# One more place for expert weights, a norm by token tile, and a scale vector loaded as rows, in a two-layer hybrid trunk

## The reference

```python
def rms_norm(x, g):
    y = x * lax.rsqrt(jnp.mean(x * x, axis=-1, keepdims=True) + EPS)
    return y * g

for i in range(2):
    h = rms_norm(x, norm_mix_g[i])
    mix = s5_mixer(h, ...) if i == 0 else diff_attention(h, w_qkv, ...)   # q, k, v = split(h @ w_qkv, 3)
    x = x + mix
    h = rms_norm(x, norm_ffn_g[i])
    x = x + hier_moe(h, ...)
return rms_norm(x, final_norm_g)
```

## Time and profile before

| | us |
|---|---|
| median of 3 runs | 857.2 (854.8 to 857.51) |
| the profiled execution | 857.5 |
| its span, first to last instruction | 855.0 |
| TensorE busy | 726.0 |
| VectorE busy | 262.4 |
| ScalarE busy | 194.3 |
| mean granted TensorE clock | 0.932 |
| transfers | 236.32 MB, mean 276 GB/s |

### The profile page before, as it was taken

The page is one execution under the profiler, slowest core; times in us unless marked ns, Lnnn a source line. Parts: engine busy times, 40 slices in busy tenths (PEclk is TensorE's granted clock), DMA queues, the critical chain, the costliest instruction groups (busy, mean ns, idle before and its releaser), DMA issues.

```text
span 855.0 us, 15847 instructions
## 1 busy us (share of the span) xinstructions
PE 726.0 (85%) x6433; PEld 434.5 (51%) x6435; DVE 262.4 (31%) x765; ACT 194.3 (23%) x451; POOL 48.8 (6%) x48
## 2 busy tenths in 40 slices
PE   4997799989977667657999988888989999987896
PEld 4987554565543333423544544475545555544453
DVE  6868971143111011002223354425101111111112
ACT  5674603241111010002102232324101111111012
POOL 3693000000000000000000000000000000000000
PEclk9998799979999798888999998989999999999898
DMA  9632209685999999999931670061999920999991
GB/s 240 186 109 96 104 7 387 230 357 236 424 424 424 422 424 424 424 425 395 397 144 66 230 292 3 0 245 57 412 424 420 423 87 0 401 423 425 422 394 51
DMA packets 59949, 236.32 MB, mean 276 GB/s; under 512 B 20008, under 2 KB 20208, under 8 KB 35312
## 3 DMA queue, kind: packets, MB, share of 16 engines
q1 hardware_dynamic: 57968, 235.23, 69.0%
q10 hardware_dynamic: 1920, 0.24, 0.2%
HBM read 234.41 MB, written 1.05 MB: 275 GB/s over the span
## 4 chain that ended last, share of the span: by engine, by line
PE 58%; SPq 17%; DMA 12%; DVE 5%; ACT 5%; issue 2%; ACTq 0%; DVEq 0%
SPq L402 15%; PE ps L1713 10%; PE ps L1778 10%; DMA ring<-in_moe_w_down 8%; PE ps L1631 6%; PE ps L1748 6%; PE ps L1755 5%; PE ps L1695 4%; DMA work<-in_moe_w_down 3%; PE ps L1502 2%; PE ps L1841 2%; PE ps L1472 2%; PE ps L1851 2%; PE ps L1662 1%; DMA work<-in_norm_mix_g 1%
## 5 line engine op out<-in xcount | busy, mean ns | idle before, releaser
L1713 PE MATMUL ps<-ring,work 128*32 128x256 f32 x1600 | 113.6, 416 | 34.9 <-DMA ring<-in_moe_w_up 22.8
L1713 PEld LDWEIGHTS ps<-ring,work 128*32 128x32 f32 x1600 | 63.2, 120 | 78.1 <-issue 55.4
L1292 DVE TENSOR_TENSOR work<-ps,work 128x256 f32<-128x256 f32 x21 | 12.9, 615 | 292.6 <-PE ps L1713 292.6
L1713 PE MATMUL ps<-work 128*32 128x256 f32 x992 | 81.9, 413 | 22.6 <-DMA work<-in_moe_w_up 11.5
L1755 PE MATMUL ps<-work 128*128 128x512 f32 x168 | 77.7, 605 | 0.0
L1748 PE MATMUL ps<-ring,work 128*32 128x512 f32 x512 | 69.1, 595 | 8.7 <-DMA ring<-in_moe_w_down 5.9
L1713 PEld LDWEIGHTS ps<-work 128*32 128x32 f32 x992 | 43.5, 119 | 59.0 <-issue 37.2
L1695 PE MATMUL ps<-work,xr 128*128 128x128 bf16 x736 | 66.6, 219 | 2.2 <-DVE work L1242 2.2
L1695 PE MATMUL ps<-work 128*128 128x128 bf16 x368 | 63.9, 219 | 0.0
L1695 PEld LDWEIGHTS ps<-work,xr 128*128 128x128 bf16 x736 | 56.5, 98 | 12.8 <-issue 8.6
L1778 PE MATMUL ps<-ring,hT 128*128 128x512 f32 x128 | 56.4, 595 | 1.7 <-ACT hT L555 1.7
(11 more groups left out here) (311 smaller groups left out, 967.6 us busy)
## 6 DMA issues: line engine op xcount, KB each, us to landing
ring<-in_moe_w_gate SPq DMA_DIRECT2D x24, 2048.0 KB, 25.0
ring<-in_moe_w_down SPq DMA_DIRECT2D x23, 2048.0 KB, 21.0
work<-in_moe_w_up SPq DMA_DIRECT2D x15, 2048.0 KB, 22.7
ring<-in_moe_w_up SPq DMA_DIRECT2D x15, 2048.0 KB, 22.8
work<-in_moe_w_down SPq DMA_DIRECT2D x8, 2048.0 KB, 27.3
work<-in_moe_w_gate SPq DMA_DIRECT2D x7, 2048.0 KB, 19.7
ring<-in_ssm_w_glu SPq DMA_DIRECT2D x4, 2048.0 KB, 8.9
ring<-in_attn_w_qkv SPq DMA_DIRECT2D x4, 2048.0 KB, 26.3
```

The source lines that it names most:

```text
L1713: ins = mm(ps[s, 6 + j // 2, 0:256], xg[:, k, s], pairs[slots[e // 2]][e % 2][:, k, :], start=(k == 0), stop=(k == KD - 1))
```

## The change

Four edits, which touch different stages:

- The scale vector of norm 0 is loaded as 8 rows of 128 into `grow`; TensorE turns it into bank 7 (one transpose ahead of `turn()`, behind a wait for the load), and ScalarE copies 8 columns to `gq[:, 0, :]`. VectorE and ScalarE wait for that copy instead of the load.
- Norm 2 goes by token tile, as norms 1 and 3 do, into banks 6, 7 (tile 0) and 4, 5 (tile 1). TensorE turns tile 0, runs `project(0, 0)`, turns tile 1, and goes on with `project(0, 1)`. `project(0, 4)` waits for hT of both tiles.
- An eleventh place, slot 10 (`SPLIT1`), is put together from x and hT. It is used in layer 1, from unit 65 on; its first use waits for `x_free`, which `residual(l, 1, 1)` raises in each layer. A unit of layer 1 from 65 on lies where the unit ten before it lay.
- `turn` and `norm` lose what was there for norm 2; the last norm is as before.

```diff
-SLOTN = 10
+SLOTN = 11
+SPLIT1 = 10
@@ slot_plan
-    order, used, plan = [(s, None) for s in TURNS] + [(LATE, None), (SPLIT, None)], list(DENSE), []
+    order, used, plan = [(s, None) for s in TURNS] + [(LATE, None), (SPLIT, None), (SPLIT1, None)], list(DENSE), []
     for i in range(2 * 6 * NQ + 8):
-        at = next(n for n, (s, _) in enumerate(order) if not (s == LATE and i in dense) and not (s == SPLIT and i >= 6 * NQ))
+        at = next(n for n, (s, _) in enumerate(order) if not (s == LATE and i in dense) and not (s == SPLIT and i >= 6 * NQ) and not (s == SPLIT1 and i <= 6 * NQ + 16))
         if i == 6 * NQ + 16:
             at = next(n for n, (s, _) in enumerate(order) if s == LATE)
+        if i == 6 * NQ + 17:
+            at = next(n for n, (s, _) in enumerate(order) if s == SPLIT1)
...
-        TURN_AT = {1: (4, 6), 3: (0, 6)}
+        TURN_AT = {1: (4, 6), 2: (6, 4), 3: (0, 6)}
...
+        halves.append((x[:].rearrange("p a n -> p (a n)"), hT[:].rearrange("p k t -> p (k t)")))
@@ SyncE, freed(i)
                     if slot == SPLIT:
                         sp.wait_ge(h_back, 4)
+                    if slot == SPLIT1:
+                        sp.wait_ge(x_free, 2)
@@ ScalarE
-            dma(gq[:, 0, :], a["norm_mix_g"][0].rearrange("(k q) -> q k", k=KD), s_gain0)
+            dma(grow[0:8, :], a["norm_mix_g"][0].rearrange("(k q) -> k q", k=KD), s_gain0)
...
             def norm(i, first):
 
                 act.activation(small[:, 40:41], con[:, C_TURN:C_TURN + 1], ACT.Sqrt)
+                act.wait_ge(scat1, first)
                 for tt in range(TT):
-                    if tt == 0:
-                        act.wait_ge(scat1, first)
-                    elif i == 2:
+                    if i == 2 and tt == 1:
                         act.wait_ge(x_new, 1)
                     square(tt, total_S[tt])
-                act.wait_ge(var_ready, VARS[i])
-                act.activation(small[:, 12:14], small[:, 10:12], ACT.Sqrt).then_inc(root_ready, 1)
-                if i < 4:
-                    act.wait_ge(hT_psum, TURNED[i])
-                    keep_turned(i, 4)
+                    if i == 2:
+                        root_tile(2, tt)
+                if i == 2:
+                    keep_tile(2, 0)
+                    keep_tile(2, 1)
+                else:
+                    act.wait_ge(var_ready, VARS[i])
+                    act.activation(small[:, 12:14], small[:, 10:12], ACT.Sqrt).then_inc(root_ready, 1)
...
-            act.wait_ge(s_gain0, 16)
+            act.wait_ge(g_psum, 1)
+            act.copy(gq[:, 0, :], ps[:, 7, 0:KD]).then_inc(g_kept, 1)
+            act.wait_ge(g_kept, 1)
             keep_turned(0, 0)
@@ VectorE, end of moe(0)
                     dve.tensor_copy(x[:, 1, :], total_S[1]).then_inc(x_new, 1)
-                    dve.wait_ge(squares, 5)
+                    var_tile(2, 0)
                     dve.tensor_copy(x[:, 0, :], total_S[0]).then_inc(x_new, 1)
                     dve.wait_ge(x_new, 2)
+                    norm_tile(2, 0)
+                    var_tile(2, 1)
+                    norm_tile(2, 1)
+                    keep_tile(2, 0)
+                    keep_tile(2, 1)
@@ TensorE
             pe.wait_ge(s_con, 16)
-            turn(0)
+            pe.wait_ge(s_gain0, 16)
+            pe.transpose(ps[:, 7, 0:KD], grow[0:KD, :], ident[0:KD, 0:KD]).then_inc(g_psum, 1)
+            turn()
...
-                residual(l, 1, 1)
+                residual(l, 1, 1).then_inc(x_free, 1)
...
             moe(0)
-            turn(2)
...
-            pe.wait_ge(hT_ready, 6)
-            pe.wait_ge(hT_late, 6)
+            turn_tile(2, 0)
+            pe.wait_ge(hT_ready, 5)
+            pe.wait_ge(hT_late, 5)
             project(0, 0)
+            turn_tile(2, 1)
             project(0, 1)
```

More of the change, by code:

```diff
@@ L51 @@
 SPLIT = 9
-DENSE = (2, 2, 1, 1, 0, 0, 0, 0, 0, 0)
+SPLIT1 = 10
+DENSE = (2, 2, 1, 1, 0, 0, 0, 0, 0, 0, 0)
 ITEMS = 32
@@ L197, in build @@
         GLU_ORDER = (0, 2, 1, 3)
-        TURN_AT = {1: (4, 6), 3: (0, 6)}
-        VARS = (1, 2, 4, 5, 7)
-        TURNED = (4, 5, 7, 8)
+        TURN_AT = {1: (4, 6), 2: (6, 4), 3: (0, 6)}
+        VARS = (1, 2, 4, 6, 8)
+        TURNED = (4, 5, 7, 9)
         o = 0
@@ L296, in build @@
             sem(n) for n in ("down_done", "y0_ready", "y1_ready", "scat0", "scat1"))
-        back_ready, x_new = sem("back_ready"), sem("x_new")
+        back_ready, x_new, x_free = sem("back_ready"), sem("x_new"), sem("x_free")
         qkv_done, qkv_kept, v_kept, qk_turned, qkT_ready = (
@@ L397, in whole @@
                 src = w[e0:e0 + 2, :].rearrange("e (p n) -> p e n", p=P)
-                if slot_of(i) == SPLIT:
+                if slot_of(i) in (SPLIT, SPLIT1):
                     for e in range(2):
-                        sp.dma_start(halves[SPLIT][e], src[:, e, :]).then_inc(here, 16)
+                        sp.dma_start(halves[slot_of(i)][e], src[:, e, :]).then_inc(here, 16)
                 else:
@@ L904, in norm @@
                 link(dve.reciprocal(small[:, 14:16], small[:, 12:14]))
-                if i == 2:
-                    for tt in range(TT):
-                        scale_tile(tt)
-                    keep_turned(2, 4)
-                else:
-                    dve.wait_ge(s_gain, 16)
-                    for tt in range(TT):
-                        STT(xr[:, tt, :, :].rearrange("p k q -> p (k q)"), total_S[tt], small[:, 14 + tt:15 + tt],
-                            gains[:, 1, :], ALU.mult, ALU.mult).then_inc(final_ready, 1)
+                dve.wait_ge(s_gain, 16)
+                for tt in range(TT):
+                    STT(xr[:, tt, :, :].rearrange("p k q -> p (k q)"), total_S[tt], small[:, 14 + tt:15 + tt],
+                        gains[:, 1, :], ALU.mult, ALU.mult).then_inc(final_ready, 1)
             def scale_tile(tt):
@@ L1454, in by_k, with turn @@
                 return x[:, tt, :].rearrange("p (q k) -> p k q", k=KD)
-            def turn(i):
-                pe.wait_ge(normed, 2 * i + 2)
+            def turn():
+                pe.wait_ge(normed, 2)
                 for b in range(4):
@@ L1471, in turn_tile @@
                 for k in range(KD):
-                    ins = mm(ps[:, TURN_AT[i][tt] + k // 4, P * (k % 4):P * (k % 4) + P], by_k(tt)[:, k, :], scales[:, tt, :],
+                    ins = mm(ps[:, TURN_AT[i][tt] + k // 4, P * (k % 4):P * (k % 4) + P], x[:, tt, P * k:P * k + P] if i == 2 else by_k(tt)[:, k, :], scales[:, tt, :],
                              start=True, stop=True)
@@ L1654, in residual @@
                 pe.wait_ge(mixed, 4 * l + 2 + 2 * tt)
-                mm(ps[:, 2 * tt + half, :], ident, x[:, tt, 512 * half:512 * half + 512], start=True, stop=True)
+                return mm(ps[:, 2 * tt + half, :], ident, x[:, tt, 512 * half:512 * half + 512], start=True, stop=True)
             def moe(l):
@@ L1864, in _ @@
             turn_qk(0, 2)
+            pe.wait_ge(hT_ready, 6)
+            pe.wait_ge(hT_late, 6)
             project(0, 4)
```

12 lines of the change are left out of this document (6 added, 6 removed).

## The result

The kernel after takes **845.5 us** (median of 4 runs, 844.76 to 846.87), the kernel before in the same comparison 857.17; the ratio is 0.9871, with a 95% interval of 0.9846 to 0.9897. A second comparison gave 846.27 us and 0.9886 (0.9868 to 0.9904). The forecast was 846.5. The profiled execution after has a span of 843.0 us, against 855.0 before.

The account below looks back on a forecast made before the run. The bound changes by stage; layer 1's three long passes wait 26.0 us for weights while transfers stand still in a hole. Slot 9.9, first norm 0.6 and norm 2 0.2 sum to 10.7: from 857.2 to 846.5 us, range 843.3 to 850.3.

Parts of the forecast that it names:

- The slot's mechanism: Layer 1's weight queue: waiting for the unit ten back instead of nine brings transfers earlier at two places.
- Rival (c): Train after the hole held by SyncE's order or ring, so the slot wins one unit only: 851.5 us, chance 0.08.
- third effect: Release behind the hole lets go unit 84, not 83, so group 6's last unit is 14th of its train: another 4.95 us.
- The term of 9.9 us: Eleventh slot in layer 1: two whole units of 4.95 us at 424 GB/s; bounds 4.95 and 10.4.
- a wait of 1.9 stays and the gain is the whole 4.95: Group 2's long pass: last down weight lands 640.3, wanted at 638.4, so the pass gains a full unit's transfer.
- reading of the three long passes: Layer 1 passes of 24.5, 23.4 and 30.6 us, against 17.5 undisturbed: the 26.0 us in excess is waiting for weights.
- rival (d): First norm: the scale row lands late and TensorE waits, 852.1 us at most; chance 0.05.
- the 4.1 of the estimate: First norm: landing time in us of the scale row, estimated from a transfer's fixed cost of about 2.0 us.
- the third bank's 15.00: First norm: the third bank lets VectorE go at 15.00 us, so the chain goes on at 17.35, 0.6 us earlier.
- My bounds, 0 and 1.5: First norm's scale row: limits in us around its forecast gain of 0.6.
- the gain of 1.8: Norm 2 by tile: projection 1 ends 1.8 us earlier if the clock is at 2.4 GHz from projection 0's start.
- the split gives nothing: Norm 2: by the skill page's clock rule, splitting the turn gives nothing; 0.2 us was taken, bounds 1.8 and -0.8.

Follow-up runs that it names:

- slot_only: The kernel before with the eleventh slot alone, from unit 65 on; 849.15 us, ratio 0.9917.
- slot_mid: The kernel before with the eleventh slot alone, first given to local unit 27 of layer 1, on which SyncE stands at the hole; 850.89 us, ratio 0.9938.
- slot_late: slot_only with the slot first given to local unit 28 of layer 1, the first issued after the hole; 857.0 us, ratio 1.0002.
- warm_start: turns_first with 20 unread products of zeros at the start and 10 of constants ahead of the first norm's turns; 841.68 us, ratio 0.983.
- warm_norm: turns_first with 22 unread filling products on TensorE ahead of norm 2's turns; 840.98 us, ratio 0.982.
- warm_both: turns_first with the fillings of warm_norm and warm_down, the latter in both passes of group 2; 842.88 us, ratio 0.984.
- warm_down: turns_first with 13 unread products ahead of the down-weight wait in both layer-1 passes of group 2; 841.68 us, ratio 0.9823.
- gain_only: The kernel before with norm 0's scale vector loaded as rows alone; 854.63 us, ratio 0.999.
- after_again: The kernel after run once more without an edit, in more rounds; 846.27 us, ratio 0.9886.
- turns_first: The kernel after with both of norm 2's tile turns ahead of projection 0; 841.81 us, ratio 0.9827.
- norm_only: The kernel before with norm 2 by token tile alone; 855.68 us, ratio 0.9993.
- warm_all: turns_first with warm_start's and warm_norm's fillings, and 13 products in group 2's first layer-1 pass only; 841.03 us, ratio 0.9827.

## Why the prediction was right, and where its terms were off

**The slot's mechanism was right.** Unit 65 left at 583.66, ahead of the release; group 2's last weight, the release behind the hole and group 6's last weight all came earlier, and what was late last stayed late last. Rival (c), one unit only, is out: slot_only and slot_mid show both units. My reading of the third effect, that the unit let go behind the hole is 84 instead of 83 because 83 has gone out before, is what slot_mid isolates; slot_late shows how little it takes to lose it.

**The term of 9.9 us was mis-sized: it brought 7.5 to 7.7.** The first unit brought 2.9 to 3.1 and not 4.95. Group 2's last weight did land nearly as much earlier as forecast, counted from the stage's release: 43.4 us after it in the kernel after against 48.2 before (636.05 - 592.62 and 645.2 - 596.99). Most of what is missing, 1.7 us, is the granted clock: six traces have the early slot and nothing filled in at group 2, and TensorE's down products there took 5.34 us in four of them and 3.64 in two. The step that failed is "a wait of 1.9 stays and the gain is the whole 4.95": I counted the wait's length and not what the clock does behind it. In the kernel before the wait right ahead of these products is 1.33 us long, and they keep 2.4 GHz; the low clock fell on the up products before them and was hidden.

The prediction's reading of the three long passes has the same gap. Not all of their 26.0 us is waiting: TensorE stands for 5.0 + 4.95 + 7.53 = 17.5 us in them, by its busy time in the earlier trace rows, and the other 8.5 are products at the low clock (0.93, 0.93 and 0.83 granted).

Where the clock held (warm_start, warm_norm), the first to the last product of hid in layer 1 took 226.3 and 226.5 us, 9.2 to 9.4 under the kernel before, close to the forecast. That difference is rough: without a gain from the slot the stretch took 235.7 to 236.7 us in four traces. The rest of what is missing is the unit: 4.7 us in slot_only, slot_mid and the kernel after, where I had 4.95 from bytes and rate, with 5.2 as the upper bound. I didn't pursue that quarter of a microsecond.

**The first norm brought 0 to 1.7 us, not 0.6.** The row landed in time in every trace that has it, so rival (d) is out. It landed at 7.30 and 7.73 in the two traces in which the transpose waited for it last (warm_both, warm_down), near the 7.3 taken from the row beside it and not at the 4.1 of the estimate. The step that failed is to take the third bank's 15.00 as fixed: that bank is TensorE's work at a pace that differs from run to run. The same 32 turning products took from 5.28 to 6.75 us. In the traces they go at 4 or 5 records in half a microsecond, the pace of norm 2's turns at 1.2 GHz, and then at 7, the pace at 2.4. The granted clock reads 1.00 all through the start, so that here the clock is read from the pace alone. Where the scale row is in, the product behind the sines follows them:

| kernel | turn, us | product behind the sines |
|---|---|---|
| gain_only | 5.28 | 16.24 |
| warm_both | 5.32 | 16.27 |
| after | 5.43 | 16.24 |
| warm_norm | 5.74 | 16.87 |
| after_again | 5.76 | 17.01 |
| warm_down | 6.30 | 17.10 |
| turns_first | 6.75 | 17.75 |

Without the row it starts at 17.54 to 17.94 in five kernels, whatever the turn took (5.41 to 6.42), since the column load sets it: 3.5 us after ScalarE has begun on the landed vector in all five. The mean gain is 17.73 - 16.78 = 0.95 us, and the ratio of gain_only gives about that. Where the turn is short the product starts at 16.24 to 16.27, since then VectorE waits for no bank and its own products before set the time; more than 1.7 wasn't to be had here. My bounds, 0 and 1.5, hold for the mean but for the wrong reason; the 1.70 between the two profiles is the lucky end. Behind it the two traces drift by the pace of other products (at 20 us 64 small ones took 2.08 us after and 3.26 before, at 65 us 32 others took 6.93 and 4.50). The 0.5 us that are left of this in the first stretch are no part of the change.

**Norm 2 by tile brought nothing.** The two profiles show 1.66 us in that stretch, and I would have booked it if the other kernels were not there. The kernel before's one trace is the odd one: its turn took 6.31 us, while slot_only, slot_late, slot_mid and gain_only, which have its norm 2 unchanged, took 5.47 and needed 36.2 to 36.5 us for the stretch. By tile it was 36.4 (norm_only), 36.6 and 36.3 (after). The forecast's mechanism was right in kind: 1.6 us of projection 0 were lost to 1.2 GHz, as the 8.67 against 7.03 shows, and they ate the gain of 1.8. The clock fell 0.7 us after the first turn had begun and rose at 408.5, 7.5 us after the turn's start: TensorE had stood for 1.2 us between. It was low for 6.8 us here, and for 3.4 in turns_first, where no such wait stood between. The Trainium skill ("TensorE: Matmul & The Clock Gate", Part 1) was cited for this: the low clock is the default and sustained activity releases it. The trace agrees in that the clock rose only within projection 0, after 3.1 us of it. From this the prediction had worked out that the split gives nothing, and turns_first shows what the split cost: with its turns together the same tile-wise norm takes 34.3 us for the stretch, 2 us less than with the split and 1.9 to 2.2 less than the norm for both tiles together took in the four kernels above.

**The sum was right partly by luck.** By the two profiles it was 2.2 us too high in one term, and 1.6 + 1.5 too low in the stretches of the two others. Against the better averaged numbers (7.5 for the slot, 0.95 for the row, 0 for the norm) the change is worth 8.5 us, or 848.7, within the range of 843.3 to 850.3 but 2 us above the forecast. The two comparisons gave 11.1 and 9.8 us by their ratios, 1.3 to 2.6 more. Of this the second interval takes in all (0.9904 is 8.2 us), the first not quite (0.9897 is 8.8 us). One place where traces differ this much is the stretch from the first GLU product to layer 0's last product of hid, which the change leaves alone but for a semaphore: it took 287.8 to 290.3 us in the fourteen traces, and the two of the kernel after are among the shortest (287.8 and 287.95). What sets it is not shown.

## What to carry to other kernels

Another buffer pays one transfer's time for each stretch in which the transfers stand still and TensorE later waits, and nothing where they never stop: look for the unit on which the queue stands when a hole begins. Where a matmul engine waits, don't cut the work behind the gap in two with another wait between: keep the short work that has to be done anyway together ahead of the long products. Here that was worth 2 us. And a gain under 2 us isn't to be read from two profiles: here the 1.7 us of one such stretch were gone as soon as four other traces with the same norm as the kernel before stood beside it.

## What was not expected of the hardware

**The clock falls or stays for the same wait.** Ahead of group 2's first down products TensorE stood for 2.10, 2.16, 2.33 and 2.39 us in the traces in which it then ran three microseconds at 1.2 GHz (the kernel after, after_again, slot_only, turns_first), and for 2.17 and 2.20 in the two in which it kept 2.4 GHz (warm_start, warm_norm). Ahead of group 5's down products, where it is off the path, it fell after waits of 1.96 to 2.60 us in nine traces and stayed after 1.48 to 1.89 in the five others (in four of these five it had been low within the up products just before). Over both places the wait's length doesn't part the two. The Trainium skill ("TensorE: Matmul & The Clock Gate", Part 1) says that the same kernel can meet the gate at another phase from run to run; the rows fit that, and no run here sets the phase. With the wait ahead of group 2's filled the products took 3.64 us in three kernels of three.

**Work that nobody reads keeps the clock.** Turns behind a filled wait took 3.84 us in warm_norm, warm_both and warm_all, against 5.46 in turns_first. At the start of the kernel, the turns behind 20 products of zeros and 10 of constants took 3.75 and 3.84, against 5.28 to 6.75. The zeros went at 0.31 us each (20 in 6.17) and the constants right behind them at 0.18 (10 in 1.80), so that the pace rose after zeros alone, with one small transpose between.
